# Five low halves made a stage earlier, and sums of squares two steps later

## What is computed

```python
def decoder_layer(x, p, ...):
    h = rmsnorm(x, g_pre_mix)
    z, q, k, v, glow, og = jnp.split(h @ w_in, SPLIT_IDX, axis=-1)
    ...
    mix = jnp.concatenate([pool_out, gla_out], axis=-1) @ w_o
    x = x + rmsnorm(mix, g_post_mix)
    f, conv_new = conv_ffn(rmsnorm(x, g_pre_ffn), conv_buf, w_up, w_conv, b_conv, w_down)
    x = x + rmsnorm(f, g_post_ffn)
    return x + (p @ w_ple) * jax.nn.sigmoid(x @ w_ple_gate)
```

## Time and profile before

| | us |
|---|---|
| median of 3 runs | 2526.17 |
| fastest, slowest | 2524.81, 2528.77 |
| profiled execution | 2530.38 |
| its span, first to last instruction | 2528.7 |

### The profile page before, as it was taken

The page is one execution under the profiler, slowest core; times in us unless marked ns, Lnnn a source line. Parts: engine busy times, 40 slices in busy tenths (PEclk is TensorE's granted clock), DMA queues, the critical chain, the costliest instruction groups (busy, mean ns, idle before and its releaser), DMA issues.

```text
span 2528.7 us, 40381 instructions
## 1 busy us (share of the span) xinstructions
PE 2505.9 (99%) x16190; PEld 2435.6 (96%) x16190; DVE 1589.8 (63%) x2516; ACT 1296.2 (51%) x1989; POOL 176.0 (7%) x508
## 2 busy tenths in 40 slices
PE   9999999999999999999999999999999999999998
PEld 8889999989999999999999999999999999999998
DVE  6678765666655556666555666655566664657865
ACT  5455554564444456444445554444564444566554
POOL 3201000100000010000001000000100000010000
PEclk9899999999999999999999999999999999999999
DMA  8335556444444645444464554446455444656565
GB/s 253 118 121 167 174 149 229 149 159 148 155 123 128 217 149 167 150 150 126 125 214 152 167 151 155 122 129 215 150 167 150 142 125 128 207 183 207 188 184 178
DMA packets 120473, 409.08 MB, mean 162 GB/s; under 512 B 12896, under 2 KB 22496, under 8 KB 119776
## 3 DMA queue, kind: packets, MB, share of 16 engines
q1 hardware_dynamic: 120288, 406.51, 51.2%
HBM read 383.56 MB, written 22.89 MB: 161 GB/s over the span
## 4 chain that ended last, share of the span: by engine, by line
PE 95%; DVE 2%; ACT 1%; DMA 1%; issue 1%; SPq 0%; DVEq 0%; ACTq 0%
PE G L1627 29%; PE G L1629 28%; PE G L1628 28%; PE X L1673 2%; PE G L1906 1%; PE G L1907 1%; PE G L1908 1%; PE X L1623 1%; PE X L1731 1%; DVE w_lo L1130 1%; PE X L1790 1%; DMA w_lo<-kept_lo 0%; PE X L1737 0%; PE X L1652 0%; PE X L1716 0%
## 5 line engine op out<-in xcount | busy, mean ns | idle before, releaser
L1627 PE MATMUL G<-h_hi,w_hi 128*128 128x384 f32 (+2 forms) x3072 | 998.8, 325 | 6.3 <-DVE w_lo L1130 3.5
L1628 PE MATMUL G<-h_hi,w_lo 128*128 128x384 f32 (+2 forms) x3072 | 989.0, 322 | 0.0
L1629 PE MATMUL G<-h_lo,w_hi 128*128 128x384 f32 (+2 forms) x3072 | 988.8, 322 | 0.0
L725 ACT ACTIVATE w_hi<-stage 128x1024 fp32r<-128x1024 f32 (+1 forms) x505 | 524.0, 1038 | 424.3 <-DMA stage<-in_w_up_units_dram 248.4
L1130 DVE TENSOR_TENSOR w_lo<-stage,w_hi 128x1024 fp32r<-128x1024 f32 (+1 forms) x505 | 605.0, 1198 | 172.4 <-ACT w_hi L725 171.6
L1627 PEld LDWEIGHTS G<-h_hi,w_hi 128*128 128x128 f32 x3072 | 580.2, 189 | 14.5 <-DVE w_lo L1130 4.7
L1628 PEld LDWEIGHTS G<-h_hi,w_lo 128*128 128x128 f32 x3072 | 580.4, 189 | 1.5
L1629 PEld LDWEIGHTS G<-h_lo,w_hi 128*128 128x128 f32 x3072 | 580.3, 189 | 0.0
L1627 PE MATMUL G<-y_hi,w_hi 128*128 128x384 f32 (+2 forms) x1056 | 342.6, 324 | 0.0
L1629 PE MATMUL G<-y_lo,w_hi 128*128 128x384 f32 (+2 forms) x1056 | 339.4, 321 | 0.0
L1628 PE MATMUL G<-y_hi,w_lo 128*128 128x384 f32 (+2 forms) x1056 | 339.3, 321 | 0.0
(11 more groups left out here) (217 smaller groups left out, 2700.6 us busy)
## 6 DMA issues: line engine op xcount, KB each, us to landing
stage<-in_w_up_units_dram SPq DMA_DIRECT2D x264, 512.0 KB, 3.6
w_lo<-kept_lo SPq DMA_DIRECT2D x107, 512.0 KB, 4.9
stage<-in_w_down_units_dram SPq DMA_DIRECT2D x96, 448.0 KB, 3.3
w_whole<-in_w_in_units_dram SPq DMA_DIRECT2D x72, 512.0 KB, 3.9
stage<-in_w_o_units_dram SPq DMA_DIRECT2D x48, 512.0 KB, 3.5
stage<-in_w_down_units_dram SPq DMA_DIRECT2D x48, 512.0 KB, 3.6
w_whole<-in_w_gate_units_dram SPq DMA_DIRECT2D x35, 512.0 KB, 3.8
stage<-in_w_in_units_dram SPq DMA_DIRECT2D x24, 512.0 KB, 4.3
```

Source lines behind the costliest of these rows:

```text
L725: act.activation(w_hi[s][:, 0:parts, :], whole[:, 0:parts, :], ACT.Copy).then_inc(hi_made, 1)
L1627: pe.matmul(ps[:, 0:w], l_hi, r_hi[:, 0:w], start=start, stop=False)
L1628: pe.matmul(ps[:, 0:w], l_lo, r_hi[:, 0:w], start=False, stop=False)
L1629: return pe.matmul(ps[:, 0:w], l_hi, r_lo[:, 0:w], start=False, stop=stop)
```

## The change

Behind the units up 8, 12, 16, 20 and 24 of tile 0 stands a new unit "halves" each, for gate units 3 to 7. It is loaded like any other, its high half is made, and its low half goes to one of two buffers `w_spare` in the region of `y_out`, which is free in tile 0. SP stores it from there. It has no matmuls; its slot is free once the low half is made. When the gate units 3 to 7 of tile 0 are due, in tile 1's passage, they load both parts as later tiles do. VectorE makes the low half of a "halves" unit two units ahead of its place, at up 7, 11, 15, 19 and 23.

The second edit: in `norm_step` of tiles 1 to 5, `add_f` of block s-4 stands where that of block s-2 stood, and those of blocks 6 and 7 move to up 0, in front of the last gating.

```diff
+HALVES_BEHIND = (8, 12, 16, 20, 24)
...
         for m in range(2 * NF):
             full(t, "up", m)
+            if t == 0 and m in HALVES_BEHIND:
+
+                units.append((t, "halves", EARLY_GATES + HALVES_BEHIND.index(m)))
...
-KEEP_LO = [unit[0] == 0 and unit[1:] in KEPT_NO for unit in UNITS]
-LOADS_LO = [unit[0] > 0 and unit[1:] in KEPT_NO and not made_again(unit) for unit in UNITS]
+KEEP_LO = [t == 0 and (kind == "in" or kind == "gate" and m < EARLY_GATES) for t, kind, m in UNITS]
+HALVES = [kind == "halves" for t, kind, m in UNITS]
+LOADS_LO = [(unit[0] > 0 or unit[1] == "gate" and unit[2] >= EARLY_GATES) and unit[1:] in KEPT_NO
+            and not made_again(unit) for unit in UNITS]
...
+        w_spare = [at(f"w_spare{j}", [P, KD, P], y_out_at + 4 * KD * P * j, F32R) for j in range(2)]
...
             def keep_los(n):
                 for k in range(keep_next[0], n + 1):
+                    if HALVES[k]:
+                        m = UNITS[k][2]
+                        sp.wait_ge(lo_made, LOS_MADE[k])
+                        sp.dma_start(kept_lo[KEPT_NO["gate", m]], exact(w_spare[spare_no(m)[0]][:, :, :])).then_inc(
+                            spare_kept[spare_no(m)[0]], 16)
...
-                    sp.wait_ge(*end_tick(UNITS[n - SLOTS]))
+                    if HALVES[n - SLOTS]:
+                        sp.wait_ge(lo_made, LOS_MADE[n - SLOTS])
+                    else:
+                        sp.wait_ge(*end_tick(UNITS[n - SLOTS]))
...
                     dve.wait_ge(hi_made, n + 1)
+                    if HALVES[n]:
+                        m = UNITS[n][2]
+                        place, count = spare_no(m)
+                        if m == EARLY_GATES:
+                            dve.wait_ge(*z_saved.at(0))
+                        if count > 16:
+                            dve.wait_ge(spare_kept[place], count - 16)
+                        dve.tensor_tensor(w_spare[place][:, :, :], stage[s][:, :, :], exact(w_hi[s][:, :, :]),
+                                          ALU.subtract).then_inc(lo_made, 1)
+                        return
...
                 if s >= 2:
                     f_rest(t, s - 2)
-                if s >= 3 and t:
-                    add_f(t, s - 2)
+                if s >= 5 and t:
+                    add_f(t, s - 4)
...
             for n, (t, kind, m) in enumerate(UNITS):
                 make_lo(n + 1)
+                if n + 2 < len(UNITS) and HALVES[n + 2]:
+                    make_lo(n + 2)
...
                     if m == 0:
                         if t:
+                            add_f(t, KD - 2)
+                            add_f(t, KD - 1)
                             gate(t - 1, KD - 1)
```

More of the change, by code:

```diff
@@ L347, in hybrid_layer @@
         kept = [sem(f"kept{s}") for s in range(SLOTS)]
+        spare_kept = [sem(f"spare_kept{j}") for j in range(2)]
         hi_made, lo_made, ticks = sem("hi_made"), sem("lo_made"), sem("ticks")
@@ L462, in keeping, with spare_no @@
             return kept[n % SLOTS], 16 * sum(KEEP_LO[k] for k in range(n % SLOTS, n + 1, SLOTS))
+        def spare_no(m):
+            return (m - EARLY_GATES) % 2, 16 * ((m - EARLY_GATES) // 2 + 1)
         def tick(name):
@@ L488, in source @@
                 return {"in": w_in_units, "o": w_o_units, "up": w_up_units, "ple": w_ple_units,
-                        "gate": w_gate_units}[kind][m]
+                        "gate": w_gate_units, "halves": w_gate_units}[kind][m]
             def keep_los(n):
                 for k in range(keep_next[0], n + 1):
+                    if HALVES[k]:
[3 more added lines that the diff above has]
+                            spare_kept[spare_no(m)[0]], 16)
                     if KEEP_LO[k]:
@@ L508, in load_unit @@
                     s = n % SLOTS
+                    if unit[0] == 0:
+                        place, count = spare_no(unit[2])
+                        sp.wait_ge(spare_kept[place], count)
                     sp.dma_start(w_whole[s][:, :, :], source(unit)).then_inc(landed[s], 16)
@@ L770, in copy_glow @@
                 act.wait_ge(*glow_made.at(t))
+                if t == 1:
+                    for m in (KD - 2, KD - 1):
+                        act.wait_ge(spare_kept[spare_no(m)[0]], spare_no(m)[1])
                 if t >= 2:
@@ L2016, in _ @@
                         sum_f(t)
-                else:
+                elif kind == "down":
                     down_part(n)
```

## The result

The kernel after the change takes 2555.16 us (median of 4 runs, 2550.93 to 2557.42), the kernel before on the same chip 2525.52. The ratio is 1.0113, interval 1.0101 to 1.0125: the change makes it 29.6 us slower. Predicted were 20.9 us more, and 2547 (2534 to 2553). The direction was right; the size was almost a third too small, and the time lies 2 us above the range. The profiled execution, the fastest of the four, lies inside the range; the other three lie above it.

A forecast was written before the change was run, and what follows sets the result against it. TensorE was taken as the bound (95% of the span), so only its waits count. Terms +12.0 - 0.8 + 8.5 + 1.2 = +20.9 us on 2526.2 gave 2547 us, range 2534 to 2553.

The forecast's parts named there:

- What bounds it: Whole kernel: TensorE, 95% of the span; in tile 1's passage VectorE, busy 28.73 of 29.20 us.
- part 1's mechanism: Tile 0's feed-forward stage: five halves units put the next low half behind gate_up; five TensorE stalls, +12.0 us.
- the walk: Hand-carried queue orders of VectorE, ScalarE, TensorE and SP through the rows; up 9 starts at 191.36 instead of 188.75.
- one landing time of 3.9 us: Tile 0's feed-forward stage: landing of the first of two loads, giving 12.3 us of stalls; 13.6 if all take 4.2.
- Part 2: Tile 1's passage: gate units load their low halves, four subtractions leave VectorE's path; alone a gain of 3.9 us.
- The net of tile 1's passage: Tile 1's passage: gain from loaded low halves, mostly eaten by the later additions; -0.8 us.
- Part 3's mechanism: Passages of tiles 2 to 4: later additions make squares wait in a ring of two; 2.8 us each, 8.5 in all.
- Tile 5: Tile 5's passage: low half of up 0 is early enough, only the sum comes late; 1.2 us.
- 2541 to 2552: Whole kernel: the forecast's own range in us, with 9 to 14 for the insertions and 6 to 10 for the later additions.
- part 1 costs only its subtractions: Rival, tile 0's feed-forward stage: insertions cost 2 us, total 2537 us; chance 0.09.
- part 3 is free: Rival, passages: the later additions cost nothing because ScalarE overtakes or is far ahead, total 2534 us; chance 0.09.
- the clock rival: Rival, waits of 2.0 to 2.7 us: each brings half clock, 1.7 us more, eight or nine of them, 2562 us; chance 0.07.

The follow-up runs named there:

- e11_two_units: Changed kernel with additions at their old steps and only two halves units (gates 6 and 7, behind up 8 and 12): 2531.45 us, 1.0016.
- e5_load_only: Kernel before plus five units behind up 8, 12, 16, 20, 24 of tile 0, only loaded, with no copies, subtractions or stores: 2536.96 us, 1.0039.
- e1_no_shift: Changed kernel with the additions of the squares back at their old steps, five halves units kept: 2540.6 us, 1.0057.
- e4_down: Changed kernel without the later additions, its five halves units moved behind down 1, 3, 5, 7 and 9 of tile 0: 2531.8 us, 1.0021.
- e9_warm_fewer: Changed kernel plus matmuls of ones filling TensorE's waits: 9 at five up units of tile 0, 24 at up 0 of tile 1: 2552.32 us, 1.0112.
- e3_ring4: Changed kernel with four buffers instead of two for the squares of a passage, additions still at the later steps: 2538.34 us, 1.0044.
- e10_before_ring: Kernel before with the later additions and four buffers for the squares, no halves units: 2524.89 us, 1.0001.
- e2_shift_only: Kernel before with the later additions alone, no halves units, two buffers for the squares: 2541.95 us, 1.0059.
- e6_warm: Changed kernel plus matmuls of ones: 14 at five up units of tile 0, 36 at up 0 of tile 1, 10 in later tiles: 2559.34 us, 1.0129.

## Why the prediction was wrong, point by point

- **What bounds it, and part 1's mechanism: right.** The five waits stand at up 9, 13, 17, 21 and 25, the low half of up 9 directly behind gate_up, e11_two_units shows that the cost comes insertion by insertion, and e5_load_only that most of it comes with the place. That it is the order on VectorE and ScalarE, as the walk has it, is seen at up 9 of the kernel after and not shown for the whole: with nothing computed up 9 waits 0.8 us and not 2.4, and later loads cost there too. The term was mis-sized: 14.5 to 14.9 us instead of 12.0, above its own range of 9 to 14. The first two insertions cost what the walk says (2.7, 2.7 to 3.0, predicted 2.6, 2.7); up 17 costs 3.6 in e1 at full clock, and behind up 25 another 1.6 us are lost at up 27 to 29, for which the walk had nothing. It took one landing time of 3.9 us for the first of two loads. ScalarE's waits for weights, tile 0's up stage (180 to 275 us), in e1:

```profile
ACT w_hi L749 <- DMA stage<-in_w_up_units_dram: 11.0, 7, 2.7
```

 The same view of before (180 to 269 us) has 7.0 us. That the landings make the difference is thus likely and wasn't tried.
- **Part 2: right in what it removes** (the waits at gates 5 to 7: -4.5 us). Alone it was to give -3.9; e1_no_shift has -0.4 with 3.4 us of half-clock loss in it, so -3.8 without (e4_down, with the same five gates, has -2.1 and a stretch of 3.4 us, again -3.8 without). The net of tile 1's passage was predicted as -0.8; it was +3.0. Of the 3.8 us between, 3.2 go when the wait is filled (e9_warm_fewer): they are the half clock behind up 0, 3.4 by its length. The step left out is that waits of 0.4 to 2.5 us at three gates and at up 0 become one of 6.4 us at up 0. The walk gives a single wait of some 3.7 us there, from which I ought to have asked about the clock: it is longer than the wait of 3.2 us that the earlier trace rows shows at half clock behind it. (Not each such wait is followed by one: the 3.4 us at up 17 of e1 weren't.) That the wait was longer still has a part in the trace that I had taken from the median of the earlier trace rows: the low half of gate 5 was issued at 539.09 and landed 6.9 us later, and ScalarE's copy waited for it, with the splits and squares behind it. ScalarE's timeline:

```profile
545.99 1.06 ACT L749 ACTIVATE w_hi<-w_whole 128x1024 fp32r<-128x1024 f32 x1 [1.73 <-DMA w_lo<-kept_lo]
...
554.90 0.52 ACT L762 ACTIVATE sq<-xr 128x384 f32<-128x384 f32 x1 [1.89 <-DVE total L1175]
...
561.41 0.52 ACT L762 ACTIVATE sq<-xr 128x384 f32<-128x384 f32 x1 [2.02 <-DVE total L1175]
```

 What that landing costs by itself wasn't tried.
- **Part 3's mechanism: right**, both waits in tiles 2 to 4, and e3_ring4 and e10_before_ring show that the two buffers are the cause. The term was mis-sized: 3.5 us for each passage (2.2 and 1.3) instead of 2.8 (its own terms of 2.0 and 0.9 add up to 2.9), 10.5 in place of 8.5. Tile 5: 1.45 for 1.2.
- **The step that failed is the clock's**, in tile 1's passage: the net of -0.8 had no half clock in it, and the runs show 3.2 to 3.4 us of it there. I made the clock a rival that is true for all waits or for none, with a chance of 0.07, since the waits of up to 2.5 us had left it whole and "the rows put these just below". Both halves of that are wrong. One wait that left it whole says nothing about others of its size: two of five waits of up to 2.6 us were followed by half clock and three were not, and of two waits of 3.4 us one was (e3_ring4) and one wasn't (e1_no_shift). And the price isn't 1.7 us for each: where TensorE waits for VectorE again some units later, most of the loss is given back there (14.5 us with no stretch, 14.9 with two, 16.2 with three). It stays where no wait follows, as behind up 0 of tile 1. That one place belonged into the sum, +3.4.
- **The sum with measured terms**: 14.9 + 3.0 + 10.5 + 1.45 = 29.9 us, against 29.6 of the medians. That they meet this closely is in part chance, as the terms are those of the profiled executions, and the others have other stretches at half clock. Of the 9.0 us above the predicted 20.9, 3.8 are in tile 1's passage (3.2 to 3.4 of them clock), 2.9 in part 1 and 2.3 in part 3. All three lay in the same direction. The second and the third alone give 2552, just inside the range of 2534 to 2553; with the first the time is outside. Parts 1 and 3 each lay above their own range too, and the prediction's "2541 to 2552" doesn't follow from these ranges: with 14 and 10 the sum is 2550.6. Tile 5's -2 in the profile stands outside this; e11_two_units, which changes nothing there, shows -1.6 at the same units.
- **The rivals.** That part 1 costs only its subtractions fell with e5_load_only, that part 3 is free with e2_shift_only: in the ring of two it isn't, with four buffers it is. That all 5.2 us of waits come in fell with the total, and the clock rival (2562) as it was put, for all waits.

No version beat the kernel before: e10_before_ring, the nearest, can't be told from it.

## What to carry to other kernels

Count the buffers before moving a consumer later: the producer stands in a first in, first out queue, and a shift by two steps in a ring of two makes it wait at every step, with all that is queued behind it (14.9 us here, nothing with four buffers). A unit inserted in a ring costs its place in the ring and in each queue more than its work: 9.8 of 14.4 us came with five that compute nothing. And where a change gathers several short waits of TensorE into a long one, with no other wait behind it, add the half clock that can follow to the sum (3.4 us here), and let the range hold both outcomes.

## What the runs showed of the hardware

- Waits of one size have different outcomes for the clock: of five waits of up to 2.6 us in one stage two were followed by a stretch at 1.2 GHz, and the 1.9 us waits in tiles 2 to 4 of the kernel after by none. A wait of 3.4 us was followed by half clock in e3_ring4 and not in e1_no_shift. What decides between them stays open.
- What half clock costs depends on the next wait. In the profiled execution of e9_warm_fewer, whose tile 2 passage has the same buffers and no added matmuls, up 0 of tile 2 grew by 3.8 instead of 2.2, with 3.4 us of half clock; but the wait for the sum that follows was gone (up 1 grew by 0.0 instead of 1.3). The passage lost 3.8 us against 3.5: of the 1.6 us, 1.3 were given back one unit later. Tiles 2 and 4 of e2_shift_only show the same.
- A low half loaded behind the whole weights of its unit took 6.9 us to land in tile 1's passage, where the median of 112 such loads is 4.9:

```profile
w_lo<-kept_lo SPq DMA_DIRECT2D x112, 512.0 KB, 4.9
```

- Filling waits with matmuls of ones (e9_warm_fewer) raised the mean clock of the four runs from 0.9945 to 0.997, and yet bought 2.8 us by the medians and nothing that the ratios show (1.0112 and 1.0113). Where the wait is shorter than the filling, the filling is the cost: in e6_warm 3.1 us at each insertion, where the kernel after waits 1.0 to 2.6.
